# Final sums: DVE adds the rows of the next tile ahead of a tile's sum from PSUM, means and scalings one tile later

## What is computed

```
out = shared(n2) + sum over the token's 6 experts of weight * expert(n2)
h   = h + g2 * out
out = h * rsqrt(mean(h*h over the 1024 columns) + 1e-6) * final_g
```

## Time and profile before

| what | value |
|---|---|
| three runs | 1284.64, 1285.57, 1287.23 us, median 1285.57 |
| profiled execution, its own time | 1287.94 us |
| profiled execution, span from first to last instruction | 1286.2 us |
| busy: TensorE / DVE / ACT / POOL | 93% / 38% / 19% / 15% |
| DMA | 334.66 MB, mean 260 GB/s |

### The profile page before, as it was taken

One profiled execution on the slowest core, in us unless ns is written; L12 is line 12 of the kernel. 1 busy time (PEld: TensorE's weight loads), 2 busy tenths in 40 slices (PEclk: granted clock), 3 DMA queues, 4 the chain that ended last, 5 costly groups with the idle time before them and its releaser, 6 DMA issues. The chain is left out here.

```text
span 1286.2 us, 13415 instructions
## 1 busy us (share of the span) xinstructions
PE 1190.0 (93%) x4799; PEld 612.6 (48%) x4799; DVE 492.2 (38%) x1007; ACT 246.1 (19%) x611; POOL 198.0 (15%) x320
## 2 busy tenths in 40 slices
PE   4999999998999999999999999999998998978884
PEld 2435864455554444448854434444443443423331
DVE  5686035654655411113765323222323232212237
ACT  2141122233432100001121212211212121211111
POOL 5000021111002000000271211122111212111101
PEclk9999999999999999999999999999999999989997
DMA  9742242213358952138157999999999999999874
GB/s 302 193 131 65 66 138 93 72 60 132 101 161 291 415 187 88 65 102 332 51 209 293 310 420 421 423 423 422 414 412 400 406 394 402 371 410 407 338 311 177
DMA packets 110985, 334.66 MB, mean 260 GB/s; under 512 B 14356, under 2 KB 67688, under 8 KB 83912
## 3 DMA queue, kind: packets, MB, share of 16 engines
q1 hardware_dynamic: 87824, 269.37, 54.7%
q0 software_dynamic: 18400, 47.10, 10.2%
q10 hardware_dynamic: 4696, 17.35, 3.3%
HBM read 314.49 MB, written 38.35 MB: 274 GB/s over the span
## 5 line engine op out<-in xcount | busy, mean ns | idle before, releaser
L1841 PE MATMUL ps<-gu_hi,xsT 128*64 128x512 f32 (+1 forms) x704 | 245.6, 623 | 24.9 <-DMA gu_hi<-in_exp_w_up_dram 10.3
L1841 PE MATMUL ps<-gu_lo,xsT 128*64 128x512 f32 (+1 forms) x320 | 148.0, 617 | 10.9 <-issue 6.7
L1841 PEld LDWEIGHTS ps<-gu_hi,xsT 128*64 128x64 f32 (+1 forms) x704 | 84.8, 156 | 136.6 <-issue 134.5
L1362 DVE SCALAR_TENSOR_TENSOR hid<-ps,wgt,gated 128x256 f32<-128x256 f32 x42 | 20.3, 484 | 306.6 <-ACT gated L940 306.6
L1849 PE MATMUL ps<-dn_hi,hidT 128*64 128x512 f32 (+1 forms) x352 | 120.6, 601 | 1.3 <-DVE hn L1358 1.1
L1488 PE MATMUL ps<-n1T,ring 128*128 128x512 f32 x256 | 111.9, 593 | 0.0
L1718 PE MATMUL ps<-n1T,ring 128*128 128x512 f32 x256 | 110.9, 592 | 0.7 <-ACT attT L880 0.7
L705 POOL DMA_INDIRECT expert_rows<-hn,meta x40 | 40.0, 1001 | 395.7 <-DVE hn L1358 352.6
L1358 DVE TENSOR_TENSOR hn<-ps,g_row 128x1024 f32<-128x1024 f32 x42 | 51.4, 1225 | 92.2 <-PE ps L1849 92.0
L1841 PEld LDWEIGHTS ps<-gu_lo,xsT 128*64 128x64 f32 (+1 forms) x320 | 51.4, 166 | 62.4 <-issue 62.0
L940 ACT ACTIVATE gated<-ps 128x256 f32<-128x256 f32 x42 | 16.1, 384 | 332.9 <-PE ps L1841 332.9
(11 more groups left out here) (336 smaller groups left out, 1353.9 us busy)
## 6 DMA issues: line engine op xcount, KB each, us to landing
gu_hi<-in_exp_w_gate_dram SPq DMA_DIRECT2D x44, 1024.0 KB, 16.0
gu_hi<-in_exp_w_up_dram SPq DMA_DIRECT2D x44, 1024.0 KB, 30.4
dn_hi<-in_exp_w_down_dram SPq DMA_DIRECT2D x44, 1024.0 KB, 27.6
ring<-in_w_in_dram SPq DMA_DIRECT2D x21, 1024.0 KB, 5.7
gu_lo<-in_exp_w_gate_dram SPq DMA_DIRECT2D x20, 1024.0 KB
gu_lo<-in_exp_w_up_dram SPq DMA_DIRECT2D x20, 1024.0 KB
dn_lo<-in_exp_w_down_dram SPq DMA_DIRECT2D x20, 1024.0 KB
h<-in_ada_w_dram POOLq DMA_DIRECT2D x32, 512.0 KB, 5.4
```

What stands on the lines that cost most here:

```text
L1841: ins = pe.matmul(ps[rows, 2 + b, :], xsT[:, b, k, rows], gu(s)[:, :, k, :], start=(k == 0), stop=(k == KC - 1))
```

## The change

DVE's loop over the four tiles is written out, with the same instructions and the same waits in another order. Addition from PSUM is `add_sums`, the mean is `mean`; `normalise` and `add_row` are as before. The rows of a tile stand ahead of the addition from PSUM of the tile before it, and mean and scaling of a tile stand behind rows and additions of later tiles. Rows 0 and 1 of tile 0 are added further up, as before. The programs of the other engines are not changed.

```
--- before.py
+++ after.py
@@ -1453,17 +1453,36 @@
                 dve.scalar_tensor_tensor(out=h[:, t, :], in0=h[:, t, :], scalar=sums[:, 8 + t:9 + t], in1=fin_g,
                                          op0=ALU.mult, op1=ALU.mult).then_inc(fin_done, 1)
 
-            for t in range(T):
-                for k in range(2 if t == 0 else 0, TOPK):
+            def add_rows(t, ks=range(TOPK)):
+                for k in ks:
                     if k not in ON_PE[t]:
                         add_row(t, k)
+
+            def add_sums(t):
                 dve.wait_ge(tail_sum, t + 1)
                 dve.tensor_tensor(h[:, t, :], h[:, t, :], flat(ps[:, 2 * t:2 * t + 2, :]), ALU.add).then_inc(fsq_in, 1)
-                if t >= 1:
-                    normalise(t - 1)
+
+            def mean(t):
                 dve.wait_ge(squares, 2 * T + t + 1)
                 dve.tensor_scalar(sums[:, 8 + t:9 + t], sums[:, 8 + t:9 + t], 1.0 / D, EPS, ALU.mult, ALU.add).then_inc(mean_done, 1)
-            normalise(T - 1)
+
+            add_rows(0, range(2, TOPK))
+            add_rows(1)
+            add_sums(0)
+            add_rows(2)
+            mean(0)
+            add_sums(1)
+            add_rows(3, range(4))
+            normalise(0)
+            mean(1)
+            add_rows(3, range(4, TOPK))
+            add_sums(2)
+            normalise(1)
+            mean(2)
+            add_sums(3)
+            normalise(2)
+            mean(3)
+            normalise(3)
 
         @block.tensor
         def _(pe):
```

## The result

The changed kernel took 1279.61 us in the median of five runs (1278.29 to 1280.38), the kernel before 1286.03 in five (1284.64 to 1287.23): 6.4 us less, a ratio of 0.995 (95% interval 0.9939 to 0.9961, that is 5.0 to 7.8 us). The profiled execution took 1278.81 us, with a span of 1277.1.

What follows compares the result with a forecast made beforehand. The tail was taken as bound by DVE's order, not its amount of work. Five tile 3 rows no longer between additions 2 and 3 save 6.28 us, other costs nothing: 1285.57 - 6.28 = 1279.3 us, range 1277.7 to 1282.0.

Steps and rivals of the forecast that it cites:

- The 5.01 us hole: DVE's wait for tile 0's PSUM sum before addition 0; tile 1's rows, 5.03 us, were to fill it.
- The 1.22 us before mean 0: DVE's wait for ACT's square of tile 0; tile 2's first row beside it was to remove the 1.22 us.
- Addition 2 stands where it stood: DVE's addition from PSUM for tile 2 keeps its time, 1266.75; five tile 3 rows no longer follow it, saving 6.28 us.
- POOL's root of tile 2: POOL's pow beside DVE's addition from PSUM: taken as 0.54 us at no cost; at 1.46 the gain is 5.78.
- The mixed case: POOL's pow beside a DVE addition with one operand in SBUF, one in PSUM; by the rule not held.
- TensorE is no later than needed: TensorE's last matmuls for tile 3 end 0.52 us before DVE's addition 3 asks, so no cost.
- Row DMAs cost nothing: Last MBs for tiles 2 and 3 land 1.5, 0.4, 0.5 and 2.0 us before DVE wants them; no cost.
- the reads start from the same event as before: Argument against the rival that rows land late by 2 us, losing 1.5 us: 1280.8 us, chance 0.10.
- POOL's drain moves with the last pow: POOL's closing 7.79 us drain starts with the last pow and moves 6.28 us earlier; rival, end unmoved, 1285.6 us, chance 0.05.
- POOL busy without showing it: Rival: each pow keeps POOL for 7.79 us, delaying the now closer pows; 3.3 us slower, 1288.9 us, chance 0.03.

Runs made afterwards that it cites:

- row moved to TensorE: Changed kernel with row 4 of tile 3 added by TensorE instead of DVE; 1280.63 us.
- half stores: Changed kernel with the root taken by ACT, the mean folded into ACT's square root, and the last tile scaled and stored in halves; 1276.88 us.
- means late only: Against the kernel before, only tile 1's rows moved ahead of mean 0; rows still follow the previous tile's addition from PSUM; 1284.03 us.
- all rows first: Changed kernel with every row addition of all tiles ahead of the first addition from PSUM; 1280.84 us.
- root on ACT: Changed kernel with the root taken from POOL: ACT takes the square root of the mean, DVE its reciprocal; 1277.37 us.

## Why the prediction was right

Forecast were 1279.3 us and a gain of 6.28; measured 1279.61 and, in the stage, 6.39.

- *The 5.01 us hole is filled by tile 1's rows*: yes, 4.97 when done alone. *The 1.22 us before mean 0 goes*: yes, 1.30 alone.
- *Addition 2 stands where it stood*, so that the gain is the five rows of tile 3: 22.46 us after the mark, against 22.55 before. The 0.09 are the one spacing that was mis-sized, as I took it from the wrong pair: from normalise 0 to mean 1 I used 1.29. In the kernel before, that spacing holds ACT's square, since the mean stood 2.43 behind its own addition from PSUM (1259.22 to 1261.65, with ACT's sum of squares there at 1261.62), as mean 2 still does after (1263.95 to 1266.38). Mean 1 now stands 7.36 behind its addition, so its square is long done, and it follows normalise 0 after 1.20 (1261.43 to 1262.63). From addition 2 to 3 it is 2.51, as worked out.
- *POOL's root of tile 2 takes 0.54, not 1.46*: 0.54. The mixed case that no row of before showed is in the trace after twice, at 0.57 and 0.54 beside an addition with one operand in PSUM, while pow 1 beside two operands in SBUF took 1.46. The row moved to TensorE changes that one neighbour: there pow 1 stands beside addition 2 and takes 0.54. By the rule of the Trainium skill ("SBUF — State Buffer", "Who interferes with whom") only the pow beside two operands in SBUF is held; the trace agrees.
- *TensorE is no later than needed*: 0.43 us to spare, 0.52 forecast; what lies beyond was shown by the row moved to TensorE.
- *Row DMAs cost nothing*: none in the changed kernel, with 0.2 us to spare for tile 3's first MB, where 0.4 was forecast. This was in part luck. Counted from the mark, the new order asks for that MB at 14.9 us, and it landed at 14.1 to 14.8 in seven of the nine profiles, but at 15.9 with the half stores, where DVE waited 0.98 us, and at 16.4 with means late only, whose order asks later. In all nine it lands 28.9 to 29.6 us after the first read of `expert_rows`; what differs is when that read goes out: 14.5 us ahead of the mark after (1226.98), 14.6 to 14.8 in six others, 13.3 and 13.1 in those two. The prediction's argument that the reads start from the same event as before does not cover this. By these numbers I estimate that in those two executions the changed order would lose 1.0 to 1.5 us, which the range allows for. Where DVE asks for it as soon as tile 2's rows are added, with all rows first, it waited 1.65.
- *POOL's drain moves with the last pow*: 7.79 us before and after. This was left open, and the root on ACT settled it: the drain starts where POOL's own list ends, not with DVE, the stores or the end of the program.
- *POOL busy without showing it*: pows 2 and 3 start 2.5 us apart after and each takes 0.54; this rival is out.
- Not forecast: the span fell by 2.7 us more than the order gave. That is scatter ahead of the mark, of which the median shows nothing: it fell by 6.42. That the median came within 0.3 us of the forecast is closer than five runs, which spread over 2.1 us, can promise.

## What to carry to other kernels

Where an engine that works in order waits at the head of its last stage while the work behind the wait is ready, the gain of a new order is the sum of its holes, up to the next engine's margin; read that margin too, since here TensorE was only 0.4 us and the DMAs 0.2 us ahead of DVE's need, and the second was gone in another execution. Compare stages from one mark, not spans, when the part ahead scatters by as much as the change. And look at what really ends the program: here POOL's drain, 7.8 us from the start of its last instruction, ended 3.1 us after SyncE had seen the last store, and a tiny job moved off POOL gave by the profile nearly half as much again (3.04 - 0.19 us) as the whole new order.

## What the runs showed of the hardware

The closing drain of POOL took 7.18 to 7.97 us in every kernel of which it is shown, also with no pow near it (7.18 us from 1228.8, with the root on ACT), while SyncE's took 7 ns and ACT's and DVE's ended with their last instruction. Where it took 7.79 us it began with the last pow; less the pow's 0.54 that leaves 7.25, close to the 7.18 without one. What these 7.2 us are, no run shows. A store of 0.25 MB took 2.2 us and one of 0.5 MB 2.6; halving the last one brought the end 0.28 us nearer to the start of the last normalise. A pow of POOL took 0.54 to 0.57 us beside an addition on DVE of one operand in SBUF and one in PSUM, and 1.39 to 1.46 beside one of two operands in SBUF.
